# Weighted one-hot rows in the expert gates: from a polynomial product to a per-partition comparison

## The reference, cut to what matters

```python
s = jnp.einsum('thpd,hpkd->thpk', q, sub_keys)              # 8 heads, 2 halves, 128 keys
s_top, i_top = lax.top_k(s, 16)
cand_s = s_top[:, :, 0, :, None] + s_top[:, :, 1, None, :]
cand_i = i_top[:, :, 0, :, None] * 128 + i_top[:, :, 1, None, :]
best_s, best_pos = lax.top_k(cand_s, 16)
experts = take_along_axis(cand_i, best_pos)                  # 8 heads x 16 = 128 per token
g = softmax(best_s)
act = gelu(einsum('thkd,td->thk', expert_u[experts], x))
out = einsum('thk,thkd->td', g * act, expert_v[experts])
```

## Time and profile before

| what | value |
|---|---|
| median of 3 runs | 2858.04 us (2856.43 to 2858.12) |
| profiled execution, its own time | 2855.57 us |
| its span, first to last instruction | 2853.7 us |
| PE busy, share of the span | 2797.1 us, 98% |
| DVE busy | 1461.0 us, 51% |
| ACT busy | 984.9 us, 35% |
| POOL busy | 1130.3 us, 40% |
| granted TensorE clock, mean | 0.994 |

### The profile page before, as it was taken

How to read it: one execution, slowest core, us unless ns; L and a number is a source line. 1 busy time by engine, 2 the same in 40 slices (tenths; PEclk the granted TensorE clock), 3 DMA queues, 4 the chain that set the end, 5 groups by cost and what they waited for, 6 DMA issues and landing times.

```text
span 2853.7 us, 37822 instructions
## 1 busy us (share of the span) xinstructions
PE 2797.1 (98%) x12895; PEld 2291.8 (80%) x12936; DVE 1461.0 (51%) x2474; ACT 984.9 (35%) x1525; POOL 1130.3 (40%) x473
## 2 busy tenths in 40 slices
PE   7999998999999999999999999999999999999998
PEld 3888887888888888887888888888786788888886
DVE  5158332299927777761555555555624642522202
ACT  4263333333334444442322222222333432332221
POOL 2305443345543333334444444444441254444442
PEclk9999999999999999999999999999999999999999
DMA  6227333244454455456667666666431133233331
GB/s 239 71 92 274 128 96 96 85 145 145 146 179 170 172 217 190 174 179 221 192 193 193 193 194 194 193 192 191 135 107 47 40 115 94 91 103 96 96 96 59
DMA packets 249964, 416.19 MB, mean 146 GB/s; under 512 B 147792, under 2 KB 148688, under 8 KB 247696
## 3 DMA queue, kind: packets, MB, share of 16 engines
q1 hardware_dynamic: 227440, 370.46, 41.4%
q10 hardware_dynamic: 20880, 36.45, 3.5%
q0 software_dynamic: 1552, 8.13, 0.8%
HBM read 345.38 MB, written 69.60 MB: 145 GB/s over the span
## 4 chain that ended last, share of the span: by engine, by line
PE 94%; DVE 3%; issue 1%; ACT 1%; DMA 0%; POOL 0%; SPq 0%; DVEq 0%; ACTq 0%; POOLq 0%
PE bank L1106 23%; PE bank L1108 22%; PE bank L1107 22%; PE pair L1108 6%; PE pair L1107 6%; PE pair L1106 6%; PE pair L1383 2%; PE bank L1248 1%; PE bank L1166 1%; PE bank L1374 1%; PE pair L1227 1%; PE bank L1237 1%; PE pair L1339 1%; PE bank L1542 0%; DVE OT L2044 0%
## 5 line engine op out<-in xcount | busy, mean ns | idle before, releaser
L581 POOL TENSOR_TENSOR wlo<-wraw,whi 128x1024 fp32r<-128x1024 f32 x456 | 1122.9, 2464 | 1589.8 <-ACT whi L651 1589.7
L1106 PE MATMUL bank<-HH,whi 128*128 128x512 f32 x2048 | 827.1, 404 | 12.9 <-DVE HL L1675 6.6
L1108 PE MATMUL bank<-HH,wlo 128*128 128x512 f32 x2048 | 799.7, 390 | 0.0
L1107 PE MATMUL bank<-HL,whi 128*128 128x512 f32 x2048 | 798.4, 390 | 0.0
L651 ACT ACTIVATE whi<-wraw 128x1024 fp32r<-128x1024 f32 x456 | 482.1, 1058 | 898.7 <-PE pair L1108 679.6
L2013 DVE TENSOR_TENSOR WL<-AJ,WH 128x512 fp32r<-128x512 f32 x128 | 308.5, 2410 | 333.1 <-ACT WH L913 333.1
L1106 PEld LDWEIGHTS bank<-HH,whi 128*128 128x128 f32 x2048 | 387.3, 189 | 90.4 <-issue 11.3
L1108 PEld LDWEIGHTS bank<-HH,wlo 128*128 128x128 f32 x2048 | 385.5, 188 | 82.7
L1107 PEld LDWEIGHTS bank<-HL,whi 128*128 128x128 f32 x2048 | 386.2, 189 | 79.5 <-issue 0.5
L1106 PE MATMUL bank<-WH,whi 128*128 128x512 f32 x512 | 199.9, 390 | 2.9 <-DVE WL L2013 2.9
L1108 PE MATMUL bank<-WH,wlo 128*128 128x512 f32 x512 | 199.7, 390 | 0.0
(11 more groups left out here) (363 smaller groups left out, 3403.6 us busy)
## 6 DMA issues: line engine op xcount, KB each, us to landing
wraw<-in_w SPq DMA_DIRECT2D x456, 512.0 KB, 3.6
act_dram<-actb ACTq DMA_DIRECT2D x128, 256.0 KB, 2.8
gate_dram<-GS SPq DMA_DIRECT2D x8, 4096.0 KB, 13.8
AJ<-act_dram SPq DMA_DIRECT2D x128, 256.0 KB, 2.7
GJ<-gate_dram SPq DMA_DIRECT2D x128, 256.0 KB, 3.8
adaw<-in_ada SPq DMA_DIRECT2D x32, 512.0 KB, 5.9
ada<-in_ada SPq DMA_DIRECT2D x16, 512.0 KB, 11.7
NB<-in_nab POOLq DMA_DIRECT2D x4, 1024.0 KB, 5.3
```

Source lines behind the costliest of these rows:

```text
L581: nc.gpsimd.tensor_tensor(wlo[:, slot, :, :].rearrange("p k c -> p (k c)"), wraw[:, slot, :, :].rearrange("p k c -> p (k c)"), whi[:, slot ...
L1106: pe.matmul(out_, ah, bh, start=first, stop=False, **kw)
L1107: pe.matmul(out_, ah, bl, start=False, stop=False, **kw)
L1108: return pe.matmul(out_, al, bh, start=False, stop=last, **kw)
```

## The change

The polynomial product goes, with its tables, its DRAM round trip, its matmul per step and the semaphores around it. The second index is kept for all token blocks (`selj`), transposed by TensorE as the first is (four more transposes), and copied to `JTS`, a part of `T`. In a step, `OG` is now made in eight VectorE operations of 128 columns, one for each token and part: compare `iota` with the token's j, times the gate, where j and the gate are columns of `JTS` and of `GHT` or `GLT`, read as one number per partition. The copy and the addition of a group's products (`g_group`, `g_sum`) each become one operation of 512 columns over a pair of banks, where there were two of 256.

```diff
@@ PE
-            def poly(q, n, variant, peeled=False):
-                if not peeled:
-                    pe.wait_ge(og_ready, q)
-                pe.matmul(bank[2][:, :], PL[:, n, :], variant, start=True, stop=True).then_inc(zj_done, 1)
...
-            pe.wait_ge(tile_evac, gu0)
             pe.wait_ge(gt_split, 1)
-            pe.wait_ge(sel_in, 16 * TB)
             for n in range(32):
-                poly(n, n, PR[:, 0, :], peeled=(n == 0))
                 u_half(gu0 + n // 2, n // 2 % R, n % 2)
...
             for tb in range(TB):
-                pe.transpose(bank[4][:, tb * P:(tb + 1) * P], gsel[:, tb, :], ident[:, :])
-                mm = pe.transpose(bank[3][:, tb * P:(tb + 1) * P], seli[:, tb, :], ident[:, :])
+                pe.transpose(bank[2][:, tb * P:(tb + 1) * P], gsel[:, tb, :], ident[:, :])
+                pe.transpose(bank[3][:, tb * P:(tb + 1) * P], seli[:, tb, :], ident[:, :])
+                mm = pe.transpose(bank[4][:, tb * P:(tb + 1) * P], selj[:, tb, :], ident[:, :])
@@ DVE
-                nc.vector.tensor_copy(selb[:, 0, :], selj[:, :])
-                then(nc.vector.tensor_tensor(selq[:, :], selj[:, :], selj[:, :], ALU.mult))
-                then(nc.vector.tensor_copy(selb[:, 1, :], selq[:, :]))
-                nc.vector.tensor_tensor(selb[:, 2, :], selq[:, :], selb[:, 1, :], ALU.subtract).then_inc(tk_sel, 1)
...
+            nc.vector.tensor_copy(JTS, bank[4][:, :])
...
-                nc.vector.tensor_tensor(OI[:, 4 * ring:4 * ring + 4, :], bc(iota[:, :], 1, 4),
-                                        bc(bank[3][:, bass.ds(q * 4, 4)], 2, P), ALU.is_equal)
-                v.wait_ge(zj_done, q + 1)
-                z = bank[2][:, :].rearrange("p (t j) -> p t j", j=P)
-                for w, gates in enumerate((GHT, GLT)):
-                    ins = nc.vector.scalar_tensor_tensor(OG[:, 4 * ring:4 * ring + 4, w, :], z, 0.0,
-                                                         bc(gates[:, bass.ds(q * 4, 4)].bitcast(F32), 2, P), ALU.max,
-                                                         ALU.mult)
+                ring = slice(4 * (n % 2), 4 * (n % 2) + 4)
+                nc.vector.tensor_tensor(OI[:, ring, :], bc(iota[:, :], 1, 4), bc(bank[3][:, bass.ds(q * 4, 4)], 2, P),
+                                        ALU.is_equal)
+                for t in range(4):
+                    for w, gates in enumerate((GHT, GLT)):
+                        ins = nc.vector.tensor_scalar(OG[:, 4 * (n % 2) + t, w, :], iota[:, :], JTS[:, bass.ds(q * 4 + t, 1)],
+                                                      gates[:, bass.ds(q * 4 + t, 1)].bitcast(F32), ALU.is_equal, ALU.mult)
                 ins.then_inc(og_ready, 1)
...
-                for k in range(2):
-                    v.wait_ge(g_high, q * 2 + (k + 1))
-                    t = 4 * (m % 16) + 2 * k
-                    low = bank[4 + 2 * (m % 2) + k][:, :].rearrange("p (t w j) -> p w j t", t=2, w=2)[:, 1]
-                    g = GS[:, m // 16, :, t:t + 2]
-                    ins = nc.vector.tensor_tensor(g, low, g, ALU.add)
-                ins.then_inc(g_evac, 1)
+                v.wait_ge(g_high, q + 1)
+                t = 4 * (m % 16)
+                low = pair[m % 2][:, :, :].rearrange("p b (t w j) -> p w j (b t)", t=2, w=2)[:, 1]
+                g = GS[:, m // 16, :, t:t + 4]
+                nc.vector.tensor_tensor(g, low, g, ALU.add).then_inc(g_evac, 1)
@@ ACT
-            act.dma_start(TL.bitcast(U16), A["polyl"]).then_inc(poly_in, 16)
-            act.dma_start(TR.bitcast(U16), A["polyr"]).then_inc(poly_in, 16)
...
-                for k in range(2):
-                    t = 4 * (m % 16) + 2 * k
-                    nc.scalar.activation(GS[:, m // 16, :, t:t + 2],
-                                         bank[4 + 2 * (m % 2) + k][:, :].rearrange("p (t w j) -> p w j t", t=2, w=2)[:, 0],
-                                         ACT.Copy).then_inc(g_high, 1)
+                t = 4 * (m % 16)
+                high = pair[m % 2][:, :, :].rearrange("p b (t w j) -> p w j (b t)", t=2, w=2)[:, 0]
+                nc.scalar.activation(GS[:, m // 16, :, t:t + 4], high, ACT.Copy).then_inc(g_high, 1)
```

More of the change, by code:

```diff
@@ L208, in build @@
         seli = a2("seli", [P, TB, P])
-        selj = a2("selj", [P, P])
-        selq = a2("selq", [P, P])
-        selb = a2("selb", [P, 3, P], BF)
+        selj = a2("selj", [P, TB, P])
         hs = a2("hs", [P, 2, NH])
@@ L224, in build @@
         SSc = T[:, 4:8, :].rearrange("p a b -> p (a b)").rearrange("p (n k) -> p n k", k=P)
[L225 to L228, removed]
+        JTS = T[:, 5, :]
         m1 = ExitStack()
@@ L382, in build @@
         tk_exp = sem("tk_exp")
-        tk_sel = sem("tk_sel")
         tk_gate = sem("tk_gate")
@@ L386, in build @@
         gt_split = sem("gt_split")
[L387 to L390, removed]
         og_ready = sem("og_ready")
@@ L865, in _ @@
                 act_tile(m, u, 16 * (m // 2))
[L866 to L873, removed]
             def g_group(q, m, stored=None):
@@ L1398, in _ @@
                 for n in range(32):
-                    poly(i * 32 + n, n, PR[:, bass.ds(i * 2, 1), :].rearrange("p o c -> p (o c)"))
                     u_half(i * 16 + (gu0 + n // 2), n // 2 % R, n % 2)
@@ L1941, in topk @@
                     then(nc.vector.tensor_tensor(cand, cand, bc(idx[:, w], 2, 16), ALU.mult))
-                    chosen = selj[:, :] if w else seli[:, tb, :]
+                    chosen = selj[:, tb, :] if w else seli[:, tb, :]
                     then(nc.vector.tensor_reduce(chosen.rearrange("p (h k) -> p h k", h=NH), cand, AX_X, ALU.add))
-                if tb:
-                    v.wait_ge(sel_out, 16 * tb)
-                nc.vector.tensor_copy(selb[:, 0, :], selj[:, :])
-                then(nc.vector.tensor_tensor(selq[:, :], selj[:, :], selj[:, :], ALU.mult))
-                then(nc.vector.tensor_copy(selb[:, 1, :], selq[:, :]))
-                nc.vector.tensor_tensor(selb[:, 2, :], selq[:, :], selb[:, 1, :], ALU.subtract).then_inc(tk_sel, 1)
                 v.wait_ge(tk_exp, tb + 1)
@@ L1963, in _, with onehots @@
             v.wait_ge(gt_turned, 1)
-            then(nc.vector.tensor_copy(GHT[:, :], bank[4][:, :]))
-            nc.vector.tensor_tensor(GLT[:, :], bank[4][:, :], GHT[:, :].bitcast(F32), ALU.subtract).then_inc(gt_split, 1)
+            nc.vector.tensor_copy(JTS, bank[4][:, :])
+            then(nc.vector.tensor_copy(GHT[:, :], bank[2][:, :]))
+            nc.vector.tensor_tensor(GLT[:, :], bank[2][:, :], GHT[:, :].bitcast(F32), ALU.subtract).then_inc(gt_split, 1)
             v.wait_ge(gt_split, 1)
-            def onehot_j(q, ring, peeled=False):
+            def onehots(q, n, peeled=False):
@@ L1992, in gate_blocks @@
+                t = 4 * (m % 16)
+                low = pair[m % 2][:, :, :].rearrange("p b (t w j) -> p w j (b t)", t=2, w=2)[:, 1]
+                g = GS[:, m // 16, :, t:t + 4]
+                nc.vector.tensor_tensor(g, low, g, ALU.add).then_inc(g_evac, 1)
             def gate_blocks(i, first):
                 for n in range(32):
-                    onehot_j(i * 32 + n, n % 2, peeled=(first and n < 2))
+                    onehots(i * 32 + n, n, peeled=(first and n < 2))
                     if n >= 2 or not first:
@@ L2313, in bf16_bits @@
     return ((bits + 0x7fff + (bits >> 16 & 1)) >> 16).astype(np.uint16)
-def bf16(a):
-    import numpy as np
-    return (bf16_bits(a).astype(np.uint32) << 16).view(np.float32)
 def pack(inp):
@@ L2352, in pack @@
     dec = np.stack([np.where(ahead >= 0, (1.0 - 2.0 ** (-5 - h)) ** np.maximum(ahead, 0), 0.0) for h in range(4)])
-    c = np.arange(P)
-    polyl, polyr = np.zeros((P, 32, P), f), np.zeros((P, 8, 4, P), f)
-    high = bf16(1.0 - c * c)
-    for block in range(8):
-        polyl[16 * block:16 * block + 2] = 1.0
-        polyr[16 * block, block], polyr[16 * block + 1, block] = high, 1.0 - c * c - high
-        for t in range(4):
-            for k, row in enumerate((2.0 * c, -1.0, -1.0)):
-                polyr[16 * block + 2 + 3 * t + k, block, t] = row
     bs = np.repeat(inp["gm_bs"][0].reshape(4, 2, 1, P), HD, axis=2)
@@ L2372, in pack @@
         dec=dec.astype(f), wsT=inp["gm_ws"][0].transpose(2, 0, 1),
-        polyl=bf16_bits(polyl).reshape(P, -1), polyr=bf16_bits(polyr).reshape(P, -1),
         bs=bs.reshape(4, P, P).transpose(1, 0, 2), keys=inp["peer_keys"][0].reshape(16, P, P).transpose(2, 0, 1))
```

3 lines of the change are left out of this document (removed).

## The result

The changed kernel takes 2955.33 us (median of 4 runs, 2954.11 to 2956.93), the kernel before 2857.23 us beside it (4 runs, 2856.13 to 2858.12). The ratio is 1.0343 [1.0327, 1.0358]: **98 us slower**, where 120 us had been forecast (2978 us, range 2900 to 3030).

A forecast was written before the change was run, and what follows sets the result against it. TensorE bounded the kernel; in the gate stage VectorE would take over. 128 steps x 0.94 us, less 0.3, is +120.0 us on 2855.57: 2975.6, plus 2.47 for the runs' median, 2978 us; range 2900 to 3030.

The forecast's parts named there:

- The bound: Gate stage: TensorE's step falls from 3.44 to 3.21 us, and VectorE's longer round becomes the new bound.
- The small operation: Each of VectorE's eight 128-column operations with two pointer scalars takes 0.27 us from start to start, at most 0.35.
- The lower end: Least cost of a small operation: 0.14 us, read from the same form with constants in place of pointers.
- The round: VectorE's work in one gate step: OI 0.60, eight small operations at 0.27, sum 0.60, together 3.36 us.
- The block: GpSimd's subtraction stops VectorE's SBUF-only operations: 2.26 us inside the eight (64%), 1.66 otherwise, 2.04 us in two steps.
- The sum: Gate step from VectorE's round plus GpSimd's block: (2 x 3.36 + 2.04) / 2 = 4.38 us, +0.94 against 3.44.
- Nothing for the merged copy and sum: ScalarE's two copies becoming one is worth nothing; VectorE's addition goes from 0.78 to 0.60 us within its round.
- The first: Gate stage: GpSimd's block falls mostly beside OI and the sum; step 3.89 us, 2915 us; low side's chance 0.06.
- The second: Gate stage: the eight run at the slow rate, 0.33 us each, and don't collide; 2909 us; chance 0.07.
- The third: Small operations cost more through the sequencer: 3023 us at 0.30 us each, 3074 us at 0.35; chance 0.06.
- The fourth: Small operations cost 0.14 us, pointers fetched during the operation before; TensorE bounds again, 2828 us; chance 0.08 including unchanged time.
- The fifth: TensorE's clock falls as it waits; at the lower level the step is 6.42 us, 3239 us; chance 0.03.

The follow-up runs named there:

- the last experiment: The changed kernel with constants in place of the two pointer scalars in each of the eight operations; 2826.08 us, ratio 0.9892.
- the short subtraction: The changed kernel with GpSimd's subtraction for the gate stage's 64 U tiles cut from 1024 columns to 64; 2835.53 us, ratio 0.9917.
- the iota in PSUM: The changed kernel with iota for the eight operations read from PSUM bank 2, where it is copied once; 2893.84 us, ratio 1.0123.
- the subtraction timed: The changed kernel with GpSimd's gate-stage subtractions held until a group's eight operations have ended; 2905.27 us, ratio 1.0160.

## Why the prediction was right, and where its terms were off

**The bound.** Right. TensorE's pace was to give way to VectorE's: VectorE busy 110 of 110 us, chain share up, waits turned round.

**The small operation.** 0.27 us forecast, 0.257 measured. Taking the form with two pointers at 512 columns and moving it to 128 columns by the slope of the earlier trace rows was 0.013 us too high. The lower end, 0.14 us, is what the form costs with constants (0.135 in the last experiment). The Trainium skill's formula (VectorE: DVE Perf Modes, section on the TRN2 errata) gives an estimate of 0.13 us here; the trace agrees with it for constants alone, and with two pointers it measures twice that. The sequencer's instructions cost nothing visible, as forecast: the changed kernel has the same distance in the 32 steps that lack them.

**The round.** 0.60 + 8 x 0.27 + 0.60 = 3.36 us forecast, 3.25 measured: 0.10 us from the eight, the rest from `OI` and the sum at 0.59 to 0.60.

**The block.** Forecast at 2.04 us for each subtraction, measured 116.4 us over 60, 1.94 each. The mechanism was right. The mean came out near by some luck, since the numbers in it were off in opposite directions. Forecast were 64% of the subtractions inside the eight at 2.26 us, and the others at 1.66. Measured were 48 of 60 (80%) inside, at 2.15, and 12 partly covered, at 1.11 on average: 0.8 x 2.15 + 0.2 x 1.11 = 1.94. The 2.15 are GpSimd's 2.41 us less the 0.26 that the held operation needs by itself. The forecast had taken off 0.14, read from an operation with constants and one with two SBUF inputs. The 1.11 are below 1.66 because 11 of the 12 started within the first 0.28 us of the sum, where nearly all of the 1.20 us covers them. GpSimd's start is not spread evenly over VectorE's round, as the 64% supposed. It hangs on ScalarE's rounding and so on TensorE (from 840 to 1370 us GpSimd waited 375 us for the rounding, and ScalarE 167 us for TensorE ahead of the activation), and they settle into a pattern that mostly repeats every four steps, two with a block and two without. The prediction had expected 3.4 and 5.5 us in turn. Why it settles as two and two, the runs don't show.

**The sum.** 3.25 + 1.94 / 2 = 4.22 us, against 4.38 forecast: 0.11 us a step from the round, 0.05 from the block, 128 x 0.16 = 20 us of the 23 us by which 2978 was too high. The last group of gate matmuls ends 99.9 us later than before (1375.24 against 1275.35 us), which is 128 x 0.78; the span grew by 98.3. The other 1.6 us were gained behind the stage, where no run says by what; the forecast had nothing there.

**Nothing for the merged copy and sum.** Right, shown alone: 0.9998 [0.9988, 1.0007].

**The rivals.** The first, mostly covered blocks, didn't happen by itself; holding GpSimd's start gave it, at 2905 us (2915 forecast with the 0.27). The second fell with the short subtraction and with the iota in PSUM. The third, a dearer small operation, didn't happen. The fourth needs constants. The fifth, a falling clock, happened in part: the prediction took a granted clock of 1.00 and named a clock that leaves it as a sign of being wrong; measured was 0.94 (the last section shows it). That step of the working failed without harm, since TensorE had slack in the stage: the fall cost nothing that these runs could find.

**What was missed** besides is an expectation within the experiments: that an extra matmul changes nothing. It gave 11 to 14 us back.

## What to carry to other kernels

Before replacing operations with a PSUM source by ones that live in SBUF alone, look at what GpSimd does meanwhile: here each of its subtractions of 2.41 us then stopped VectorE for up to 2.23 us, and everything queued behind waited with it. Of the two costs of this change, the many small operations (eight at 0.26 us) would still have left a gain of some 23 us; the lost PSUM source turned it into a loss, and a difference written to PSUM in each step (five operations of 512 columns) keeps the gain of the removed matmul. Where a collision can't be avoided, its price hangs on the moment, and a wait that fixes the other engine's start ahead of PSUM work is worth some 50 us here.

## What was not expected of the hardware

**The clock fell after waits of about 2 us, though not after each.** TensorE in the changed kernel after a wait of 1.97 us, timeline:

```profile
993.68 0.39 PE L1082 MATMUL bank<-HH,wlo 128*128 128x512 f32 x1
996.03 0.96 PE L1352 MATMUL pair<-OG,OI 128*128 128x256 f32 x4 [1.97 <-DVE GS L1946]
996.79 0.63 PE L1080 MATMUL bank<-HH,whi 128*128 128x512 f32 x1
997.22 0.63 PE L1081 MATMUL bank<-HL,whi 128*128 128x512 f32 x1
...
999.35 0.57 PE L1080 MATMUL bank<-HH,whi 128*128 128x512 f32 x1
999.76 0.39 PE L1081 MATMUL bank<-HL,whi 128*128 128x512 f32 x1
```

Matmuls of 512 columns start 0.43 us apart from 996.79 to 999.35, and 0.23 us apart later: half the rate, the level of 1.2 GHz. The window 995 to 1000 us shows it as 0.66, its neighbours are at 1.00 in the windows above. From 840 to 1370 us TensorE has 30 waits of 1.87 to 2.08 us, each for VectorE, and 21 of them have such a slow stretch right behind. With the extra matmul the waits are shorter: of 30 waits of 1.56 to 1.82 us one, the longest, is followed by a slow stretch, and the window 945 to 1055 us was at 0.98. With the subtraction timed, waits are about 1 us and the clock 1.00. The prediction leaned on the earlier trace rows, where TensorE was busy 6.43 of 8 us at 1.00. The one long wait there took 1.57 us, so the row had the right share of busy time but not the waits of 2 us that this kernel has.

**GpSimd gets in between operations that VectorE has back to back.** At 1003.57 it started 0.15 us into one small operation; the next, at 1003.67, was the one held. Each of the 60 subtractions read in the stage has its long distance, so VectorE's row of eight never kept GpSimd out for its whole length; the subtractions themselves are recorded at 2.36 to 2.55 us.

**Pointer scalars have a price:** 0.12 us for two of them in one operation of 128 columns, nearly as much as the operation itself (0.135 us). The sequencer's instructions that set them, recorded at 93 ns each, add nothing to the distance.
